# One transformer block and two layers with a top-k expert lookup on one core: query weights of four heads kept in four gather slots

## The chip, the cores and the metric

The program runs on one core of a Trainium2 chip. A core has a matrix engine (TensorE, PE in the profile, with its weight loads as PEld), a vector engine (VectorE, DVE), a scalar engine (ScalarE, ACT), a general engine that issues the gathers (GpSimd, POOL) and one that issues the other transfers (SyncE, SP). Sixteen DMA engines move data between HBM and the on-chip memory (SBUF, 128 partitions). Results of matmuls stand in PSUM. The metric is the device time of one execution in microseconds, and the median over runs is compared.

## The reference

`x` (256 x 1024) goes through one block with differential and grouped attention, then through a product-key expert lookup, and then through two layers with a Fourier branch, windowed attention and a gated feed-forward. Everything is float32. The part that matters here is the lookup:

```python
def one(xc):                      # 128 tokens
    q = (xc @ w_q).reshape(C, PEER_HEADS, 2, PEER_HALF)              # 8 heads, 2 x 128
    s = jnp.einsum('chpd,hpnd->chpn', q, subkeys, ...)
    sv, si = lax.top_k(s, PEER_TOPK)                                 # 16 of 128, twice
    cand = sv[:, :, 0, :, None] + sv[:, :, 1, None, :]
    best, pos = lax.top_k(cand.reshape(C, PEER_HEADS, 256), PEER_TOPK)
    ids = ...                                                        # 16 experts per token and head
    g = jax.nn.softmax(best, axis=-1)
    ue = jnp.take(u, ids, axis=0); ve = jnp.take(v, ids, axis=0)     # rows of 1024 each
    a = jax.nn.gelu(jnp.einsum('cd,chkd->chk', xc, ue), approximate=False)
    return jnp.einsum('chk,chkd->cd', (g * a), ve)
```

Each of 256 tokens and 8 heads takes 16 rows of `u` and of `v`, 4 KB each: 268 MB in all.

## The kernel before

**Stages.** The kernel first does the block (modulation, input projections, attention, output projection, second norm), then 16 stages of the lookup, then the two layers. A stage is one head for one half of the tokens (128 tokens, one to a partition); stage n works on tokens c = n % 2 of head n // 2. `NC` is 2, `PH` 8, `TOPK` 16, `STAGES` 16.

**One stage.** `u` and `v` stand side by side in `uv`, so one gather fetches for each of 128 partitions a row of 2048 floats (8 KB), 1.05 MB in all. POOL issues 16 gathers (`gather`, L759). VectorE takes the dot product of the `u` half with the token (`dot`, L2199, recorded on L2202), 16 times, and after every 4 of them a small product (`weights`). ScalarE does the gelu of those 4 (L1677) and from each weight a diagonal matrix (L1681, four buffers). TensorE multiplies each diagonal matrix with the `v` half and adds it up in PSUM (`experts`, L1159, recorded on L1166), and adds one to `pair_free` when a pair is done. `pair_free` stands at NS = 16 when the first stage begins.

**Slots.** There are NS = 16 slots of 8 KB per partition. Slots 0 to 7 are halves of the four quarters of `ring`, the buffer in which every other weight lands (`pairs_at`, L237); slots 8 to 15 are in `arena`, where the attention kept its data. `FIRST_SLOTS` (L87) says which slot takes gather k of a stage: the five arena slots 8 to 12 first. In the first stage a gather waits for whatever used its slot before; in later ones gather k waits for the same k of the stage before.

**Queries.** Head h needs 1 MB of query weights in `wqb`, which SP loads when the queries of head h - 1 are done (`q_done`, L726 to L729), and TensorE takes them in `all_queries(h)` (L1134) and writes the scores (`all_key_sums`). VectorE finds the 16 best (`topk`), which is needed one stage ahead. ScalarE copies the queries out of PSUM (`query_out`) and does the softmax (`softmax`, L1645), for which another activation table is loaded than for gelu. The orders of the work on each engine are written out by hand, and the middle heads are loops (`Fori`).

**Ends.** The modulation weights come first, in four slots of 2 MB. TensorE sums the first four of eight row blocks in float32 from the raw slot (`mod_raw`, L838, L840). The others are split by ScalarE (`first_high`, L448) and VectorE (`first_rest`, L454) into a high part and a remainder and multiplied in `mod_parts`. In the layers every weight piece of 1024 columns is split in the same way: `weight_high` on ScalarE (L557), `weight_rest` on VectorE (L572). SP loads the first layer slots (`lslot(0)` to `lslot(3)`, the four quarters of `ring`) at L731 to L738, one after the other.

## Time and profile before

| what | value |
|---|---|
| median of 3 runs | 1478.48 us (1478.26 to 1478.79) |
| the profiled execution | 1479.35 us, its span 1477.5 us |
| mean granted TensorE clock | 0.964 |
| busy share: PE, DVE, ACT, POOL | 90%, 73%, 41%, 19% |
| moved by gathers | 268.45 MB, 36,864 packets |
| moved by SP's loads | 146.82 MB |

The shares are means over three stretches. Until 227 us the block is computed, between 227 and about 888 us the lookup, and the rest are the two layers, about 290 us each. The page cuts the span in 40 slices of 37 us, and a share or rate of one slice tells more than the mean. Rates of transfer are over all sixteen DMA engines.

### The profile page before, as it was taken

The page shows a single profiled execution, that of the slowest core. Times are in us where ns is not written, and L with a number is a line of the kernel's source. Part 1 is how long each engine was busy: PE and PEld are TensorE (multiplying, and loading weights), DVE is VectorE, ACT ScalarE, POOL GpSimd, SP SyncE. Part 2 cuts the span into 40 slices and gives each one's busy share as a digit, 9 for nine tenths or more (in the row PEclk, how much of TensorE's full clock was granted, in tenths as well). Part 3 has the DMA queues.
Part 4 walks back from the last instruction along what each step waited for, and adds up shares of the span by engine and source line. Part 5 has one row for each costly group of instructions (what it writes and reads, how often), then busy time and mean ns, then how long its engine had stood idle before and what let it go on. Part 6 is the DMA issues. An engine that isn't in the chain of part 4 may idle for free.

```text
span 1477.5 us, 18644 instructions
## 1 busy us (share of the span) xinstructions
PE 1335.6 (90%) x6216; PEld 917.7 (62%) x6216; DVE 1077.9 (73%) x2271; ACT 601.4 (41%) x1234; POOL 281.5 (19%) x263
## 2 busy tenths in 40 slices
PE   8998899998797979798897788999999999999998
PEld 3876664543342424253343346679999876899987
DVE  5698857876767677776777777878887577788864
ACT  5343643212222222212132226566665455666652
POOL 0000004554433334444444220000000000000000
PEclk9999999999898989899898899999999999999999
DMA  9624437999999999999999996434445433345530
GB/s 395 261 114 170 173 138 324 421 421 422 421 422 422 422 422 422 422 422 422 422 421 422 421 401 258 171 114 172 172 172 200 161 144 126 115 178 195 197 145 29
DMA packets 49847, 416.21 MB, mean 282 GB/s; under 512 B 5488, under 2 KB 5616, under 8 KB 7024
## 3 DMA queue, kind: packets, MB, share of 16 engines
q0 software_dynamic: 36864, 268.45, 43.7%
q1 hardware_dynamic: 12912, 146.82, 26.1%
q8 instruction: 44, 0.72, 0.2%
q14 instruction: 27, 0.22, 0.0%
HBM read 414.20 MB, written 1.05 MB: 281 GB/s over the span
## 4 chain that ended last, share of the span: by engine, by line
PE 54%; DMA 16%; DVE 14%; issue 9%; POOL 5%; ACT 2%; POOLq 0%; DVEq 0%; SPq 0%; ACTq 0%
DMA ring<-in_uv,ids 13%; PE ps L1166 7%; PE ps L1454 6%; PE ps L1453 6%; PE ps L1455 6%; PE ps L1245 4%; PE ps L1247 4%; PE ps L1246 4%; POOL arena L762 3%; POOL ring L762 2%; DVE arena L2202 2%; PE ps L989 2%; PE ps L878 2%; PE ps L880 2%; PE ps L879 2%
## 5 line engine op out<-in xcount | busy, mean ns | idle before, releaser
L1166 PE MATMUL ps<-arena 128*128 128x512 f32 x512 | 254.7, 653 | 93.2 <-ACT arena L1681 92.7
L1166 PEld LDWEIGHTS ps<-arena 128*128 128x128 f32 x512 | 105.2, 210 | 235.5 <-issue 124.8
L572 DVE TENSOR_TENSOR arena_r<-ring,arena_r 128x1024 fp32r<-128x1024 f32 x152 | 185.1, 1223 | 60.7 <-ACT arena_r L557 60.2
L762 POOL DMA_INDIRECT arena<-in_uv,ids x128 | 137.6, 1075 | 479.1 <-issue 256.4
L1166 PE MATMUL ps<-ring,arena 128*128 128x512 f32 x512 | 225.6, 593 | 2.7 <-ACT arena L1681 1.6
L2202 DVE CUSTOM_DVE_ANT_0 ring<-ring,arena 128x1024 f32<-128x1024 f32 x128 | 153.1, 1222 | 70.8 <-DMA ring<-in_uv,ids 67.5
L1453 PE MATMUL ps<-hH,arena_r 128*128 128x256 f32 x704 | 199.4, 283 | 0.0
L1455 PE MATMUL ps<-hH,arena_r 128*128 128x256 f32 x704 | 199.2, 283 | 0.0
L1454 PE MATMUL ps<-arena_r 128*128 128x256 f32 x704 | 199.2, 283 | 0.0
L2202 DVE CUSTOM_DVE_ANT_0 arena<-arena 128x1024 f32<-128x1024 f32 x128 | 153.3, 1224 | 57.1 <-DMA arena<-in_uv,ids 55.0
L557 ACT ACTIVATE arena_r<-ring 128x1024 fp32r<-128x1024 f32 x152 | 158.8, 1052 | 58.8 <-PE ps L1247 58.6
L1166 PEld LDWEIGHTS ps<-ring,arena 128*128 128x128 f32 x512 | 96.9, 190 | 124.5 <-issue 119.0
L762 POOL DMA_INDIRECT ring<-in_uv,ids x128 | 143.3, 1119 | 108.5 <-PE ps L1166 74.5
L1681 ACT ACTIVATE arena<-cst,wts 128x128 f32<-128x128 f32 x256 | 89.5, 394 | 145.7 <-DVE wts L2196 73.6
L1454 PEld LDWEIGHTS ps<-arena_r 128*128 128x128 f32 x704 | 135.2, 192 | 0.0
L1453 PEld LDWEIGHTS ps<-hH,arena_r 128*128 128x128 f32 x704 | 135.2, 192 | 0.0
L1455 PEld LDWEIGHTS ps<-hH,arena_r 128*128 128x128 f32 x704 | 135.2, 192 | 0.0
L1677 ACT ACTIVATE gel<-dots 128x4 f32<-128x4 f32 (+2 forms) x68 | 13.9, 205 | 207.9 <-DVE dots L2202 207.7
L1245 PE MATMUL ps<-arena_r 128*128 128x512 f32 x240 | 94.9, 395 | 1.7 <-DVE arena_r L627 1.6
L1247 PE MATMUL ps<-arena_r 128*128 128x512 f32 x240 | 93.5, 390 | 0.0
L1246 PE MATMUL ps<-arena_r 128*128 128x512 f32 x240 | 93.5, 389 | 0.0
L1837 ACT ACTIVATE arena<-ps,lps 128x256 f32<-128x256 f32 x88 | 49.8, 566 | 96.6 <-DVE arena L2465 56.9
(334 smaller groups left out, 2041.8 us busy)
## 6 DMA issues: line engine op xcount, KB each, us to landing
ring<-in_lw SPq DMA_DIRECT2D x39, 2048.0 KB, 7.7
ring<-in_b1w SPq DMA_DIRECT2D x18, 2048.0 KB, 8.8
wqb<-in_wq SPq DMA_DIRECT2D x8, 1024.0 KB, 9.0
ring<-in_lw SPq DMA_DIRECT2D x8, 1024.0 KB, 5.1
ring<-in_lw SPq DMA_DIRECT2D x2, 1088.0 KB, 10.6
arena<-in_uv,ids POOLq DMA_INDIRECT x128
ring<-in_uv,ids POOLq DMA_INDIRECT x128, 22.0
cst<-in_const SPq DMA_DIRECT2D x1, 1487.5 KB, 22.1
```

The costliest lines, as they stand in the source:

```text
L557: nc.scalar.activation(high_of(l, p), piece_raw(p), ACT.Copy).then_inc(w_hi, 1)
L572: nc.vector.tensor_tensor(low_of(l, p), piece_raw(p), high_of(l, p).bitcast(F32), ALU.subtract)\
L762: pool.indirect_dma_start(pairs_at[at], None, uv, bass.IndirectOffsetOnAxis(ap=ids[:, c, k:k + 1], axis=0))\
L1166: last = nc.tensor.matmul(ps[:, 4 + 2 * c + b, :], diag[:, k % 4, :], vrows[at[k]][:, b * 512:(b + 1) * 512], start=False, stop=(close and ...
L1245: nc.tensor.matmul(dst, ah, high_of(l, p)[:, cols_], start=first, stop=False, skip_group_check=True)
L1246: nc.tensor.matmul(dst, ah, low_of(l, p)[:, cols_], start=False, stop=False, skip_group_check=True)
L1247: last = nc.tensor.matmul(dst, al, high_of(l, p)[:, cols_], start=False, stop=end, skip_group_check=True)
L1453: nc.tensor.matmul(dst, high, hH[:, k, :], start=(k == 0), stop=False)
L1454: nc.tensor.matmul(dst, high, hL[:, k, :], start=False, stop=False)
L1455: last = nc.tensor.matmul(dst, low_of(l, p)[:, k * P:(k + 1) * P], hH[:, k, :], start=False, stop=(k == KD - 1))
L1681: nc.scalar.activation(diag[:, k % 4, :], ident, ACT.Copy, scale=wts[:, c, k:k + 1])\
L2202: V.tensor_tensor_reduce(out=urows[at], in0=urows[at], in1=hrow[:, c, :], scale=1.0, scalar=0.0, op0=ALU.mult, op1=ALU.add, accum_out=dots ...
```

## The change

Six edits stand in one diff.

1. `SLOTS` lists twelve slots, and gather k of stage n takes slot `SLOTS[(16 n + k) % 12]`, so it waits for the pair twelve before it. Slots 8 to 11 take no gathers.
2. These four areas (`kept_wq`) take the query weights of heads 1 to 4. SP loads them when the attention's scores (`sc_done`) and its transposes (`pt_done`) are done. Heads 5 to 7 go through `wqb` as before, the first of them when head 0's queries are done.
3. The loops over heads are written out on all engines.
4. The first four slots of modulation weights are loaded as halves; `mod_raw` waits for the first half (`half_in`), everything else for both.
5. In the head loop ScalarE does the second softmax ahead of `query_out`; at the end of the lookup it loads the table for square roots behind three weight pieces and not ahead of them. SP's loads of the first layer slots wait for the last use of both halves of a quarter.
6. In the layers, `weight_rest` of pieces 5 to 7 stands behind `rotation`, and that of piece 9 behind the two products with `rstd`.

```diff
@@ -84,9 +84,21 @@
 GROUP = 4
-FIRST_SLOTS = (8, 9, 10, 11, 12, 0, 1, 2, 3, 4, 5, 13, 14, 15, 6, 7)
+SLOTS = (12, 3, 0, 1, 2, 4, 5, 13, 14, 15, 6, 7)
+KEPT = 4
 GROUPS = TOPK // GROUP
 STAGES = NC * PH
+
+
+def place(n, k):
+    return SLOTS[(TOPK * n + k) % len(SLOTS)]
+
+
+def turn_of(n, k):
+    return (TOPK * n + k) // len(SLOTS) + 1
+
+
+LAST_USE = {at: g + 1 for g in range(TOPK * STAGES) for at in (SLOTS[g % len(SLOTS)],)}
 ENDS = tuple(GROUP * (g + 1) for g in range(GROUPS))
@@ -237,6 +249,7 @@
         hrow = area(64, NC, D)
+        kept_wq = [area(8 * i, KD, 256) for i in range(KEPT)]
         diag = area(72, 4, P)
@@ -528,7 +543,7 @@
             elif l == 0 and p < 2:
-                act.wait_ge(pair_free, NS + TOPK * (STAGES - 1) + 12)
+                act.wait_ge(q_done, PH)
             elif l == 0 and p < 4:
@@ -711,7 +726,10 @@
                 w = 2048 if n == IN_SLOT[1] else SLOT
-                sp.dma_start(ring[:, n % RING, 0:w], b1w[n, :, 0:w]).then_inc(slot_in[n % RING], 16)
+                at = SLOT // 2 if n < MOD_A else 0
+                if at:
+                    sp.dma_start(ring[:, n, 0:at], b1w[n, :, 0:at]).then_inc(half_in[n], 16)
+                sp.dma_start(ring[:, n % RING, at:w], b1w[n, :, at:w]).then_inc(slot_in[n % RING], 16)
                 if n == 1:
@@ -723,14 +741,18 @@
             sp.dma_start(skb[:, :], sk).then_inc(sk_in, 16)
-            with sp.Fori(1, PH) as h:
-                sp.wait_ge(q_done, h)
-                sp.dma_start(wqb[:, :, :], wq[bass.ds(h, 1), :, :].rearrange("a p (k n) -> (a p) k n", k=KD))\
-                    .then_inc(wq_in, 16)
-
-            sp.wait_ge(pair_in[NS - 2], 16 * STAGES)
+            sp.wait_ge(sc_done, 16)
+            for i in range(KEPT):
+                if i == 2:
+                    sp.wait_ge(pt_done, 16)
+                sp.dma_start(kept_wq[i], wq[i + 1, :, :].rearrange("p (k n) -> p k n", k=KD)).then_inc(kept_in[i], 16)
+            for h in range(KEPT + 1, PH):
+                sp.wait_ge(q_done, 1 if h == KEPT + 1 else h)
+                sp.dma_start(wqb[:, :, :], wq[h, :, :].rearrange("p (k n) -> p k n", k=KD)).then_inc(wq_in, 16)
+
+            sp.wait_ge(pair_in[place(STAGES - 1, TOPK - 2)], 16 * turn_of(STAGES - 1, TOPK - 2))
             for j in range(RING):
-                sp.wait_ge(pair_free, NS + TOPK * (STAGES - 1) + 2 * j + 2)
+                sp.wait_ge(pair_free, NS + max(LAST_USE[2 * j], LAST_USE[2 * j + 1]))
                 if j == 0:
@@ -757,26 +779,23 @@
 
-            def gather(n, c, k, at):
+            def gather(n, c, k):
+
+                at = place(n, k)
                 pool.sem_inc(pool_passed, 1)
...
 
-            def stage(n, c):
-
-                pool.wait_ge(ids_ready, n + 1)
-                pool.sem_inc(pool_passed, 1)
-                for k, at in enumerate(FIRST_SLOTS):
-                    pool.wait_ge(pair_free, TOPK * n + k + 1)
-                    gather(n, c, k, at)
-
             pool.wait_ge(first_ids, 1)
             pool.sem_inc(pool_passed, 1)
-            for k, at in enumerate(FIRST_SLOTS):
+            for k in range(TOPK):
+                at = place(0, k)
                 if k == 8:
                     pool.wait_ge(ids_ready, 1)
-                if at == 0:
+                if k >= len(SLOTS):
+                    pool.wait_ge(pair_free, NS + k - len(SLOTS) + 1)
+                elif at == 3:
                     pool.wait_ge(wo_used, 4)
@@ -784,17 +803,13 @@
                     pool.wait_ge(q_done, 1)
-                gather(0, 0, k, at)
-            stage(1, 1)
-            with pool.Fori(1, PH - 1) as i:
-                stage(i * 2, 0)
-                stage(i * 2 + 1, 1)
-            stage(STAGES - 2, 0)
-            pool.wait_ge(ids_ready, STAGES)
-            pool.sem_inc(pool_passed, 1)
-            for k in range(TOPK):
-                pool.wait_ge(pair_free, TOPK * (STAGES - 1) + FIRST_SLOTS.index(k) + 1)
-                gather(STAGES - 1, 1, k, k)
+                gather(0, 0, k)
+            for n in range(1, STAGES):
+                pool.wait_ge(ids_ready, n + 1)
+                pool.sem_inc(pool_passed, 1)
+                for k in range(TOPK):
+                    pool.wait_ge(pair_free, NS + TOPK * n + k - len(SLOTS) + 1)
+                    gather(n, n % NC, k)
 
@@ -835,7 +850,7 @@
 
-                wait_slot(pe, i)
+                pe.wait_ge(half_in[i], 16)
                 for k in range(4):
@@ -1133,10 +1148,14 @@
 
-                pe.wait_ge(wq_in, 16 * h + 16)
+                if h <= KEPT:
+                    pe.wait_ge(kept_in[h - 1], 16)
+                else:
+                    pe.wait_ge(wq_in, 16 * (h - KEPT + 1))
+                head = kept_wq[h - 1] if h <= KEPT else wqb
                 for s in range(2):
                     for k in range(KD):
-                        last = nc.tensor.matmul(ps[:, 0, s * S:(s + 1) * S], wqb[:, k, s * P:(s + 1) * P], hT[:, k, :],
+                        last = nc.tensor.matmul(ps[:, 0, s * S:(s + 1) * S], head[:, k, s * P:(s + 1) * P], hT[:, k, :],
                                                 start=(k == 0), stop=(k == KD - 1))
@@ -1687,11 +1706,11 @@
             experts(0, 0, groups=range(1, GROUPS))
-            with act.Fori(0, PH - 2) as i:
+            for i in range(PH - 2):
                 softmax(i * 2 + 2, 0)
                 experts(i * 2 + 1, 1)
+                softmax(i * 2 + 3, 1)
                 query_out(i + 2)
-                softmax(i * 2 + 3, 1)
                 experts(i * 2 + 2, 0)
@@ -1702,8 +1721,6 @@
 
-            table(ACT.Sqrt)
-
             def squares_of(c):
@@ -1711,6 +1728,7 @@
             weight_high(act, 0, 0, 1, 2)
+            table(ACT.Sqrt)
             block_high(act, 1, range(4))
@@ -2196,18 +2214,19 @@
 
-            def dot(n, c, k, at):
-
-                dve.wait_ge(pair_in[at], 16 * n + 16)
+            def dot(n, c, k):
+
+                at = place(n, k)
+                dve.wait_ge(pair_in[at], 16 * turn_of(n, k))
                 V.tensor_tensor_reduce(out=urows[at], in0=urows[at], in1=hrow[:, c, :], scale=1.0, scalar=0.0,
...
 
-            def products(n, c, ends=ENDS, at=FIRST_SLOTS):
+            def products(n, c, ends=ENDS):
 
...
                     for k in range(start, end):
-                        dot(n, c, k, at[k])
+                        dot(n, c, k)
                         if k == start and g > 0:
@@ -2320,8 +2337,6 @@
 
-                weight_rest(dve, l, *range(5, P_O - 2))
-
                 def rotation(i, gain):
@@ -2349,16 +2364,18 @@
                 rotation(1, lpv(l, "kn"))
+                weight_rest(dve, l, *range(5, P_O - 2))
                 fold_fourier()
...
                 variance(20, HD)
-                weight_rest(dve, l, P_O - 2, P_O - 1)
+                weight_rest(dve, l, P_O - 2)
                 newton(20, l * 4 + 8)
...
                     run(V.tensor_tensor(r3, r3, rstd[:, r0:r0 + nh].unsqueeze(2).broadcast_to([P, nh, HD]), ALU.mult))
+                weight_rest(dve, l, P_O - 1)
                 for c in range(NC):
```

The loops on TensorE and VectorE are written out in the same way (`for i in range(...)` in place of `Fori`), and `experts` takes its slot from `place(n, k)`.

On GpSimd, the first gathers of the lookup, before: `first_ids`, `wo_used`, `ids_ready`, `mod_used`, `q_done` are what a gather waits for, and `arena` and `ring` say in which kind of slot it lands.

```order
9 L762 DMA arena<-in_uv,ids 128x2048 [waits first_ids]
10 L762 DMA arena<-in_uv,ids 128x2048 x4
11 L762 DMA ring<-in_uv,ids 128x2048 [waits wo_used]
12 L762 DMA ring<-in_uv,ids 128x2048 x2
13 L762 DMA ring<-in_uv,ids 128x2048 [waits ids_ready]
14 L762 DMA ring<-in_uv,ids 128x2048 [waits mod_used]
15 L762 DMA ring<-in_uv,ids 128x2048
16 L762 DMA arena<-in_uv,ids 128x2048 [waits q_done]
17 L762 DMA arena<-in_uv,ids 128x2048 x2
18 L762 DMA ring<-in_uv,ids 128x2048 [waits mod_used]
```

The same place on GpSimd in the changed kernel, up to the first gather that waits for a freed pair:

```order
9 L786 DMA arena<-in_uv,ids 128x2048 [waits first_ids]
10 L786 DMA ring<-in_uv,ids 128x2048 [waits wo_used]
11 L786 DMA ring<-in_uv,ids 128x2048 x3
12 L786 DMA ring<-in_uv,ids 128x2048 [waits mod_used]
13 L786 DMA ring<-in_uv,ids 128x2048
14 L786 DMA arena<-in_uv,ids 128x2048 [waits q_done]
15 L786 DMA arena<-in_uv,ids 128x2048 [waits ids_ready]
16 L786 DMA arena<-in_uv,ids 128x2048
17 L786 DMA ring<-in_uv,ids 128x2048 [waits mod_used]
18 L786 DMA ring<-in_uv,ids 128x2048
19 L786 DMA arena<-in_uv,ids 128x2048 [waits pair_free]
```

Before, five gathers stand ahead of the first that waits for the output projections (`wo_used`); now one does, and the thirteenth already waits for a pair.

On SyncE, from the last loads of the block to the first layer slots, before (`wqb` and `skb` are the queries' and keys' weights, `pair_in14` the landing in slot 14; the loop of L726 runs seven times):

```order
20 L723 DMA wqb<-in_wq 128x2048 [waits modcol_done]
21 L725 DMA skb<-in_sk 128x2048 [waits in_used]
22 L726 UNCONDITIONAL_BRANCH
23 L728 ISA [waits q_done]
24 L728 DMA wqb<-in_wq 128x2048
25 L726 REGISTER_ALU
26 L726 COMPARE_AND_BRANCH
27 L735 DMA ring<-in_lw 128x2048 [waits pair_free,pair_in14]
28 L736 DMA ring<-in_lw 128x2048
```

The same on SyncE in the changed kernel (`pair_in0` is the landing in slot 0, gather 14 of the last stage):

```order
26 L741 DMA wqb<-in_wq 128x2048 [waits modcol_done]
27 L743 DMA skb<-in_sk 128x2048 [waits in_used]
28 L748 DMA arena<-in_wq 128x2048 [waits sc_done]
29 L748 DMA arena<-in_wq 128x2048
30 L748 DMA arena<-in_wq 128x2048 [waits pt_done]
31 L748 DMA arena<-in_wq 128x2048
32 L751 DMA wqb<-in_wq 128x2048 [waits q_done] x3
33 L757 DMA ring<-in_lw 128x2048 [waits pair_free,pair_in0]
34 L758 DMA ring<-in_lw 128x2048
```

Four loads of query weights moved to the attention's end and three stay behind `q_done`; the first layer load now waits in `pair_free` for pair 256, the last of all, where it waited for the second pair of the last stage.

## Rows read from the trace of the kernel before

**Rows 1.** The page, rate of transfer in 40 slices of 37 us.
```profile
GB/s 395 261 114 170 173 138 324 421 421 422 421 422 422 422 422 422 422 422 422 422 421 422 421 401 258 171 114 172 172 172 200 161 144 126 115 178 195 197 145 29
```
**Rows 2.** Transfer queues in 390 to 750 us: packets, MB, share of 16 engines.
```profile
q0 software_dynamic: 20281, 147.69, 98.5%
q1 hardware_dynamic: 576, 4.19, 2.8%
```
**Rows 3.** Timeline, VectorE (start, length), the last dots of stages 4 and 5.
```profile
442.40 1.23 DVE L2202 CUSTOM_DVE_ANT_0 ring<-ring,arena 128x1024 f32<-128x1024 f32 x1 [1.25 <-DMA ring<-in_uv,ids]
...
482.12 1.23 DVE L2202 CUSTOM_DVE_ANT_0 ring<-ring,arena 128x1024 f32<-128x1024 f32 x1 [1.25 <-DMA ring<-in_uv,ids]
```
**Rows 4.** Timeline, TensorE, the last transposes of the attention's probabilities.
```profile
201.59 0.60 PE L956 MATMUL ps<-cst,arena 128*128 128x128 f32 x4
```
**Rows 5.** Stretches: length, busy us and count of each engine, PEclk, DMA share, GB/s.
```profile
210.00:227.00 17.00, 16.10 (x78) 10.29 (x79) 13.13 (x54) 6.12 (x14) 0.00 (x0) 1.00 0.00 1
...
229.00:231.00 2.00, 2.00 (x6) 0.94 (x5) 1.83 (x8) 0.10 (x1) 1.55 (x2) 1.00 0.72 164
```
**Rows 6.** Timeline, GpSimd, the first and the sixth gather.
```profile
227.75 1.08 POOL L762 DMA_INDIRECT arena<-in_uv,ids  x1 [226.61 <-issue]
...
234.54 1.36 POOL L762 DMA_INDIRECT ring<-in_uv,ids  x1 [0.30 <-issue]
```
**Rows 7.** The chain of waits: TensorE behind the output projections.
```profile
233.56 4.45 PE ps L813 x11
```
**Rows 8.** Issue to landing: the sixth gather alone, then all of L762.
```profile
ring<-in_uv,ids POOLq DMA_INDIRECT x1, 12.1
...
DMA to landing us min/median/max: 9.4/22.0/25.0
```
**Rows 9.** Timeline, GpSimd at the first freed pair of stages 5 and 6, and TensorE.
```profile
466.88 0.94 POOL L762 DMA_INDIRECT arena<-in_uv,ids  x1 [13.30 <-PE ps L1166]
...
508.07 0.94 POOL L762 DMA_INDIRECT arena<-in_uv,ids  x1 [13.95 <-PE ps L1166]
...
472.86 10.46 PE L1166 MATMUL ps<-ring,arena 128*128 128x512 f32 x24
```
**Rows 10.** Timeline, ScalarE, the table load ahead of gelu in stage 6.
```profile
501.26 1.28 ACT L1677 ACT_TABLE_LOAD   x1
```
**Rows 11.** The chain of waits at the start; then a stretch as in rows 5.
```profile
3.62 20.20 DMA ring<-in_b1w
23.87 6.24 PE ps L840 x8
...
24.00:26.00 2.00, 2.00 (x3) 0.26 (x2) 1.97 (x6) 1.85 (x2) 0.00 (x0) 0.50 0.99 426
```
**Rows 12.** Timeline, VectorE, after the remainders of the third slot.
```profile
31.85 0.54 DVE L1949 TENSOR_SCALAR arena<-ps,sm 128x256 f32<-128x256 f32 x1 [3.24 <-ACT arena_r L1523]
```
**Rows 13.** The chain of waits, the first weights of layer 0.
```profile
885.64 5.05 DMA ring<-in_lw
```
**Rows 14.** Timeline at the join: VectorE, TensorE, VectorE.
```profile
888.12 1.23 DVE L2202 CUSTOM_DVE_ANT_0 arena<-arena 128x1024 f32<-128x1024 f32 x1 [0.75 <-DMA arena<-in_uv,ids]
...
890.33 1.98 PE L1166 MATMUL ps<-arena 128*128 128x512 f32 x4 [0.36 <-ACT arena L1681]
...
892.91 1.23 DVE L572 TENSOR_TENSOR arena_r<-ring,arena_r 128x1024 fp32r<-128x1024 f32 x1 [3.07 <-ACT arena_r L557]
```
**Rows 15.** Timeline of layer 0: VectorE, VectorE, ScalarE.
```profile
911.26 3.50 DVE L572 TENSOR_TENSOR arena_r<-ring,arena_r 128x1024 fp32r<-128x1024 f32 x3 [2.46 <-ACT arena_r L557]
...
918.89 1.21 DVE L2354 TENSOR_REDUCE sm<-arena 128x16 f32<-128x1024 f32 x1
...
917.22 1.04 ACT L1752 ACTIVATE arena<-arena 128x1024 f32<-128x1024 f32 x1
```
**Rows 16.** Queues in 866 to 876 us, and VectorE's longest wait in it.
```profile
q14 instruction: 1, 0.01, 0.2%
...
873.30 1.22 DVE L2202 CUSTOM_DVE_ANT_0 arena<-arena 128x1024 f32<-128x1024 f32 x1 [2.29 <-DMA arena<-in_uv,ids]
```

More of the change, by code:

```diff
@@ L324, in program @@
         slot_in = [sem(f"slot_in{i}") for i in range(RING)]
+        kept_in = [sem(f"kept_in{i}") for i in range(KEPT)]
+        half_in = [sem(f"half_in{i}") for i in range(MOD_A)]
         act_step, dve_step, passed, pool_passed = sem("act_step"), sem("dve_step"), sem("passed"), sem("pool_passed")
@@ L1181, in _ @@
             keys(2)
-            with pe.Fori(1, PH - 2) as i:
+            for i in range(1, PH - 2):
                 experts(i * 2, 0)
@@ L2223, in _ @@
             for k in range(GROUP):
-                dot(0, 0, k, FIRST_SLOTS[k])
+                dot(0, 0, k)
             dve.wait_ge(prob_done, 1)
@@ L2230, in _ @@
             for k in range(GROUP, TOPK):
-                dot(0, 0, k, FIRST_SLOTS[k])
+                dot(0, 0, k)
                 if k % 4 == 0 and k > GROUP:
@@ L2236, in _ @@
             dve.wait_ge(row_out, 4)
-            with dve.Fori(0, PH - 1) as i:
-                chain.enter(i, 2 * (4 * 3 + 1 + 7 + 1))
+            for i in range(PH - 1):
                 topk(i * 2 + 2, i + 1, 0)
@@ L2242, in _ @@
                 products(i * 2 + 2, 0)
-                chain.leave(PH - 1)
             dve.wait_ge(mod_out, MODS)
```

10 lines of the change are left out of this document (5 added, 5 removed).

## The prediction, written before the changed kernel was run

> **What bounds the kernel now.** I read the slices of the page first. From about 227 us to 885 us the transfers stand at 421 to 422 GB/s without a break [rows 1], and between 390 and 750 us the gathers alone fill 98.5% of the sixteen engines [rows 2]. A gather is 128 rows of 8 KB, 1.05 MB, so it costs 1.0486/0.422 = 2.485 us of this stream, and so does each head's 1 MB of query weights that goes through it. One head (two stages of 16 gathers and one weight load) is 33 x 2.485 = 82.0 us. VectorE shows the same: the last gather of one stage lands at 442.40, that of the next at 482.12 [rows 3], 39.7 us apart, 16 x 2.485. In this stretch no engine's work has a price unless it leaves the stream empty; bytes and starts have. Before and behind it the chain of waits runs through TensorE, VectorE and ScalarE.
>
> **Removed bytes.** Seven weight loads stand in the stream (heads 1 to 7). Afterwards it holds three (heads 5 to 7); the other four go out once the attention scores and transposes are done. The last attention transposes end at 202.2 [rows 4], and between 210 and 227 us the transfers run at 1 GB/s [rows 5]: 4 MB fit in with room. Gain: 4 x 2.485 = **-9.9 us**. No query waits for them, as these land well before 227.
>
> **The first gathers.** Now five gathers go into the arena before anything from the ring is needed (POOL issues from 227.75, every 1.24 us, and the sixth at 234.54 without having waited [rows 6]). Afterwards only one does; the second goes to slot 3, which is free when both output projections are done. TensorE's next work starts at 233.56 [rows 7], and POOL follows a release by 0.8 us: 234.4. The stream really fills up 2.4 us after the first issue (164 GB/s in 229 to 231, 0 before, [rows 5]), at about 230.2. The gather of 234.54, sixth in line, lands 12.1 us later [rows 8], at 246.6; 230.2 + 6 x 2.485 is 245.1, so completion adds 1.5, and a gather that finds the stream empty lands after 2.4 + 2.5 + 1.5 = 6.4 us. The second gather then lands at 240.8 and not at 230.2 + 2 x 2.485 + 1.5 = 236.7: **+4.1 us**. If the second start is as quick as the queue latency inside a busy stream it could be 2, not less than 1.5; and not over 5.
>
> **Twelve slots and not sixteen.** Gather k of a stage is now let go by the pair twelve before. The tight ones are k = 12 to 15, which wait for the stage's own first four pairs. In the odd stage shown, the previous stage's last gather landed at 442.40, and POOL issued what the first freed pair released at 466.88, 24.5 us later [rows 3, 9]; gather 12 is due 13 x 2.485 = 32.3 us after 442.40. It has 7.8 us, against the 6.4 just worked out, and the three behind it are freed every 1.74 us (24 matmul records for six pairs in 10.46, [rows 9]) and due every 2.49. In the even stage POOL comes 508.07 - 482.12 = 26.0 later [rows 3, 9], but there the softmax stands behind the copy of the queries, and so the softmax, its table load and gelu's table load of 1.28 us, which ends at 502.54 [rows 10], all fall between the dots and gelu. With the softmax ahead of the copy one load of 1.28 and the 0.4 of the softmax leave this path, and 24.3 us remain. So the stream stays full, with 1.4 us to spare: **0**. What is not known is the lead a transfer needs with only three ahead of it; the smallest that the trace shows is 9.4 us, the median 22.0 [rows 8], and both are queueing. That is the rival below. Moving the softmax has no other price: TensorE's key sums wait for the copy, but its next pair waits for gelu anyway.
>
> **First weights as halves.** The third slot of modulation weights lands at 3.62 + 20.20 = 23.82 and TensorE's eight row sums start on it at 23.87; they take 6.24 us [rows 11]; between 24 and 26 us the granted clock is 0.50, the level of 1.2 GHz, after TensorE had stood still for 1.8 us. The first half lands 2.5 us earlier, at 21.3. Then they are done by 27.6 even at the lower clock. Whole slots are still awaited by ScalarE's splitting, so VectorE's remainders don't move; but VectorE idles 3.24 us until 31.85 for ScalarE, which waits for TensorE behind these sums [rows 12]. That idle time is what can go: **-3.2 us**, 2.4 if the clock falls all the same, 0 if a later transfer sets the end (the trace has no DMA wait between 40 and 227, so I take 3.2). It shifts everything up to the first gather.
>
> **The join to layer 0.** This is what the new order costs. 256 gathers over twelve slots end on slots 12, 3, 0, 1. Slots 0 and 1 are the ring quarter of the first layer weights, and SP issues all four quarters in order. Now SP issues at 885.64, before the last pair is even read, and the first MB lands 5.05 us later [rows 13], 2.6 after the last dot began at 888.12. Afterwards it must wait for the last pair's matmuls, 890.33 + 1.98 = 892.3 [rows 14], so it lands at 892.4 + 5.05 = 897.4 on the old clock. VectorE's remainder of the first piece stands ahead of the residual in program order and starts 1.1 us behind ScalarE's start on it: 898.6 and not 892.91 [rows 14], **+5.7 us**. The table load moved behind three pieces gains nothing, since there is no data at that time. TensorE now stands still for 7.7 us instead of 2 and may start at the lower clock; its work there is paced by VectorE (2.7 us a piece), so I count 0, at most 2.
>
> Where a rule stands beside this: the Trainium skill (TensorE: Matmul & The Clock Gate, "HAM oscillation — how this bites in real kernels") says that a DMA wait of some microseconds sends TensorE back to the lower clock. By it the join would cost up to 2 more. The row of 24 to 26 us agrees that a pause has that effect.
>
> **Reordered remainders.** Layer by layer VectorE idles 2.46 us until 911.26 for ScalarE; the four rotation products (1.7 us) move in front of that wait. The norm's reduction starts at 918.89, ScalarE's square for it ends at 918.26 [rows 15]. So 0.6 is to be had, less 0.2 for the last piece that now comes later to TensorE: **-0.8 us** for both layers (-1.4 to 0).
>
> **Unrolled loops.** The loops hold their code: in 390 to 750 us no instruction queue appears among the queues [rows 2]. Written out, some 3,000 further instructions must be fetched through the same engines. At 64 bytes that is 0.2 MB, 0.5 us of stream if spread. 
> **Sum:** -9.9 + 4.1 - 3.2 + 5.7 - 0.8 + 1.0 = -3.1 us. The profiled execution took 1479.35 (span 1477.5), 0.9 over the median of 1478.48, so I forecast 1479.35 - 3.1 = 1476.2 for one like it and **1475.4** for the median. 0.2% is 3.0 us, about what can be told from no change, so the forecast lies on that edge.
>
> **Rivals.** (1) *The stream is cheaper than thought:* the second start costs 2 and not 4, fetches cost nothing, TensorE's earlier end carries over. -9.9 + 2 - 3.2 + 5.7 - 1.4 = -6.8: 1471.7. For it: the second start falls on engines already warm. Against: the join is arithmetic. (2) *Twelve slots starve the stream (slower):* in each of 13 stages gather 12 arrives late by what its lead exceeds 7.8 us. At 8.6 us it is 0.8 x 13 = 10.4, 1478.5 - 3.1 + 10.4 = 1485.8; at the 9.4 of rows 8 it is 21, 1496. It decides from 8.0 us on. For it: no gather in the trace had a lead under 9.4. Against: those were queued behind others, and 6.4 follows from the first six. The Trainium skill (DMA: Bandwidth & Descriptors, "Anatomy of one DMA — SWDGE (gpsimd) path") gives 2.0 us plus size over 436 GB/s, 4.4 us for a gather; by that the margin is 3.4 and this rival falls. (3) *The join and the fetches are dearer* (2 for the clock, 5 for fetches): -3.1 + 2 + 4 = +2.9: 1481.4. (4) *The early part does not carry over*, the weights' halves being hidden: +3.2, 1478.6, which I count with (3).
>
> **Chances.** Forecast 0.60 (its own range 1472.5 to 1478; 0.36 of it faster, 0.24 within 0.2%), (1) 0.17 faster, (2) 0.12 slower, (3) and (4) 0.11 (0.06 within, 0.05 slower). Faster 0.53, same 0.30, slower 0.17. The range 1469.5 to 1483 reaches into (1) and (3) and leaves out most of (2).
>
> **What would show it.** VectorE's wait of 3.24 us near 30 us gone and the first gather near 224.5; the second gather 6.6 us behind it; three weight loads after 240; 422 GB/s in every slice of the stream, and no waits for a landing longer than 1.3 us; the last dot near 879; first layer weights landing 9.3 us behind the last dot's start and not 2.6; the layers shorter by under 1 us. A stream below 420 GB/s in the middle would make the forecast wrong upward, a first gather still at 227.7 by 3 us.

## The result: 0.17% slower, and the profile after

The changed kernel takes 1481.45 us (median of 20 runs, 1480.51 to 1482.94), the kernel before in the same sessions 1478.88 (20 runs, 1478.26 to 1480.3). The ratio is 1.0017 with a 95% interval of 1.0011 to 1.0024: slower by some 2.6 us, where the forecast was 3.1 us faster. The profiled span is 1480.3 us against 1477.5, 2.8 us more, and I split them at four points.

| stretch | before | after | change | forecast |
|---|---|---|---|---|
| start to first gather's issue | 227.75 | 224.57 | -3.2 | -3.2 |
| to the last dot of stage 1 | 317.18 | 315.56 | +1.6 | +4.1 - 2.5 |
| to the last dot of all | 888.12 | 885.17 | -1.3 | -7.5 + 1.0 |
| to the first remainder of layer 0 | 892.91 | 896.80 | +6.8 | +5.7 |
| to the end of the span | 1477.5 | 1480.3 | -1.1 | -0.8 |

Columns two and three are where the stretch ends. The second point in both kernels, in VectorE's timeline, before and then after:

```profile
317.18 1.22 DVE L2202 CUSTOM_DVE_ANT_0 ring<-ring,arena 128x1024 f32<-128x1024 f32 x1 [1.24 <-DMA ring<-in_uv,ids]
...
315.56 1.23 DVE L2221 CUSTOM_DVE_ANT_0 arena<-arena 128x1024 f32<-128x1024 f32 x1 [1.25 <-DMA arena<-in_uv,ids]
```

The first two lines and the last came close to what was worked out; the fourth cost 1.1 us more. The third is where the forecast broke: three weight loads of 2.485 us are gone from it, and it is shorter by 1.3 us only.

The early part, in timelines of the kernel after (start, length, idle before and its releaser):

```profile
28.47 0.99 DVE L1967 TENSOR_SCALAR arena<-ps,sm 128x256 f32<-128x256 f32 x2
...
224.57 1.08 POOL L786 DMA_INDIRECT arena<-in_uv,ids  x1 [223.44 <-issue]
231.21 0.94 POOL L786 DMA_INDIRECT ring<-in_uv,ids  x1 [5.55 <-PE ps L1004]
```

The wait of 3.24 us at 31.85 [rows 12] is gone; the same operation now follows its predecessor at 28.47 without a wait. The first gather goes out 3.2 us earlier than in [rows 6], and the second stands 5.55 us behind TensorE's output projection.

The transfers, from the page, then from the queues in 390 to 750 us, then stretches (length, busy time and count of PE, PEld, DVE, ACT, POOL, granted clock, DMA share, GB/s):

```profile
GB/s 392 263 114 209 157 226 317 421 421 422 421 421 418 421 411 422 412 411 421 418 420 409 413 349 257 170 115 163 180 171 192 158 119 160 114 176 192 199 145 29
```

```profile
q0 software_dynamic: 20322, 148.00, 99.4%
q1 hardware_dynamic: 288, 2.10, 1.4%
q8 instruction: 6, 0.10, 0.1%
q14 instruction: 10, 0.08, 0.1%
```

```profile
390.00:750.00 360.00, 297.56 (x763) 144.10 (x763) 253.81 (x631) 84.27 (x217) 148.99 (x141) 0.94 1.01 417
...
816.00:850.00 34.00, 25.89 (x53) 11.29 (x54) 24.08 (x51) 6.51 (x21) 13.75 (x12) 0.80 1.01 412
```

In [rows 1] every slice of the stream shows 421 or 422; now there are slices of 409 to 413. In [rows 2] no instruction queue appears; now two do, with 16 packets and 0.18 MB, which is 0.4 us of stream. The bytes are nothing, and yet 1% of the rate is missing. In the landing times of the gathers there is a regular step of 2.49 us. Eight times between 390 and 888 us one gather of the changed kernel lands 0.94 to 0.97 us later than this step, and the following ones keep the delay. Each stands 2.1 to 3.3 us behind an 8 KB packet of instructions on q14:

```
fetch on q14 (us)   403.9  452.3  524.1  571.0  646.6  696.9  769.6  818.0
next late landing   406.24 454.40 527.41 573.04 648.63 699.31 772.29 820.63
later by            0.97   0.97   0.97   0.94   0.97   0.97   0.95   0.96
```

Six other 8 KB packets on q14 in this stretch (445.9, 471.9, 607.4, 653.4, 765.9 and 831.0 us) have no step behind them. The trace of before has one such step between 390 and 888 us, that of [rows 16], and one more at 330.5; the changed kernel has a small one of 0.27 at 335.7. So the table's third stretch has six full steps and 0.27 more than before, 6.0 us, against the 6.2 by which -1.3 misses the three loads' -7.5. So far this is a coincidence in time; whose fetches they are, and whether twelve slots matter, was for the experiments.

The join, in the chain of waits of the kernel after, and VectorE's timeline:

```profile
869.20 21.28 PE ps L1185 x47
890.54 5.15 DMA ring<-in_lw
895.72 1.06 ACT arena_r L572
```

```profile
885.17 1.23 DVE L2221 CUSTOM_DVE_ANT_0 ring<-ring,arena 128x1024 f32<-128x1024 f32 x1 [0.70 <-DMA ring<-in_uv,ids]
...
896.80 1.23 DVE L587 TENSOR_TENSOR arena_r<-ring,arena_r 128x1024 fp32r<-128x1024 f32 x1 [9.91 <-ACT arena_r L572]
...
915.21 3.50 DVE L587 TENSOR_TENSOR arena_r<-ring,arena_r 128x1024 fp32r<-128x1024 f32 x3 [0.98 <-ACT arena_r L572]
```

The load leaves 5.4 us behind the start of the last dot; in [rows 13, 14] it left 2.5 us ahead of it. VectorE stands for 9.91 us where it stood for 3.07. Further on its wait of 2.46 us [rows 15] is 0.98.

### The profile page after: what moved, and what is told of

It is laid out like the page before. It is cut to its first block, busy times and chain, and to the rows that moved or that the text cites. A ratio compares the mean times of both kernels' runs of the same rounds, so it can differ in the third digit from the quotient of the medians.

```text
span 1480.3 us, 17546 instructions
## 1 busy us (share of the span) xinstructions
PE 1335.9 (90%) x6216; PEld 916.7 (62%) x6216; DVE 1076.5 (73%) x2271; ACT 598.9 (40%) x1234; POOL 279.4 (19%) x263
## 3 DMA queue, kind: packets, MB, share of 16 engines
q0 software_dynamic: 36864, 268.45, 43.9%
## 4 chain that ended last, share of the span: by engine, by line
PE 52%; DVE 22%; DMA 13%; issue 6%; ACT 3%; POOL 3%; DVEq 0%; SPq 0%; POOLq 0%; ACTq 0%
DMA ring<-in_uv,ids 8%; PE ps L1185 7%; PE ps L1472 6%; PE ps L1474 6%; PE ps L1473 6%; PE ps L1264 4%; DMA arena<-in_uv,ids 4%; PE ps L1266 4%; PE ps L1265 4%; DVE ring L2221 4%; DVE arena L2221 3%; POOL ring L786 2%; PE ps L1004 2%; PE ps L893 2%; PE ps L894 2%
## 5 line engine op out<-in xcount | busy, mean ns | idle before, releaser
L1185 PE MATMUL ps<-ring,arena 128*128 128x512 f32 x684 | 315.5, 612 | 33.2 <-ACT arena L1700 33.2
L2221 DVE CUSTOM_DVE_ANT_0 ring<-ring,arena 128x1024 f32<-128x1024 f32 x171 | 205.7, 1223 | 99.4 <-DMA ring<-in_uv,ids 99.2
L1185 PEld LDWEIGHTS ps<-ring,arena 128*128 128x128 f32 x684 | 133.7, 197 | 207.1 <-issue 163.3
L1185 PE MATMUL ps<-arena 128*128 128x512 f32 x340 | 169.3, 638 | 65.7 <-ACT arena L1700 65.7
L786 POOL DMA_INDIRECT ring<-in_uv,ids x171 | 184.2, 1077 | 192.3 <-PE ps L1185 147.1
L786 POOL DMA_INDIRECT arena<-in_uv,ids x85 | 94.7, 1114 | 394.4 <-issue 237.3
L1185 PEld LDWEIGHTS ps<-arena 128*128 128x128 f32 x340 | 66.9, 203 | 157.2 <-ACT arena L1700 82.5
L2221 DVE CUSTOM_DVE_ANT_0 arena<-arena 128x1024 f32<-128x1024 f32 x85 | 103.4, 1222 | 42.2 <-DMA arena<-in_uv,ids 41.4
```

The lines of the kernel that those rows point to most:

```text
L786: pool.indirect_dma_start(pairs_at[at], None, uv, bass.IndirectOffsetOnAxis(ap=ids[:, c, k:k + 1], axis=0))\
L1185: last = nc.tensor.matmul(ps[:, 4 + 2 * c + b, :], diag[:, k % 4, :], vrows[place(n, k)][:, b * 512:(b + 1) * 512], start=False, stop=(clo ...
L2221: V.tensor_tensor_reduce(out=urows[at], in0=urows[at], in1=hrow[:, c, :], scale=1.0, scalar=0.0, op0=ALU.mult, op1=ALU.add, accum_out=dots ...
```

## The experiments

Theory A: the instruction fetches of POOL's written-out loop delay the stream. Theory B: twelve slots starve it. Theory C: only both together. All kernels below were timed against the kernel before; the interval is that of the ratio.

### Is it POOL's code, the depth, both, or the other engines' code?

**e1**, the kernel before with POOL's loop written out:

```diff
-            with pool.Fori(1, PH - 1) as i:
+            for i in range(1, PH - 1):
```

> The kernel before with one edit: POOL's loop over the stages is written out, every other engine keeps its loop, sixteen slots. Theory A (each 8 KB instruction fetch that POOL needs for its written-out gathers puts a lasting 0.95 us into the landings of the gathers; the trace after shows eight such steps, the trace before two): about seven fetches more, 6 to 7 us slower than before, so about +0.45%, and the landings go up in steps of some 0.95 us about every 1.5 stages. Theory B (the twelve slots starve the stream, the fetches are harmless): no change, ratio 1.000. Theory C (fetches cost only together with the shallower queue): fetches appear in the trace with steps in the single landings, but the span stays within 1 us.

Measured: 1478.73 us against 1478.96, ratio 1.0000 (0.9991 to 1.0009). Its queues in 390 to 750 us and its stretch of 816 to 850 us:

```profile
q14 instruction: 2, 0.02, 0.0%
```

```profile
816.00:850.00 34.00, 24.93 (x55) 10.65 (x54) 24.88 (x56) 8.05 (x23) 8.72 (x8) 0.85 1.01 421
```

Three fetches in the whole loop (443.6, 603.7, 764.4), not the seven of the expectation, and no step behind any. Theory A falls: the eight steps of the changed kernel are not POOL's.

**e2**, the kernel before, loops and sixteen slots kept, with every gather held back by four more pairs (the first stage's last four and the last stage alike):

```diff
-                    pool.wait_ge(pair_free, TOPK * n + k + 1)
+                    pool.wait_ge(pair_free, TOPK * n + k + 5)
```

> The kernel before with one edit: sixteen slots and all loops as they are, but every gather from the thirteenth of the first stage on waits for four pairs more, so that at most twelve are in flight or in use, as in the changed kernel. Theory A (fetches of the written-out loop): no change beyond 0.5 us. Theory B (twelve slots starve the stream): 6 us slower, about +0.4%. Theory C (both together): no change here, slow packets rare.

Measured: 1480.17 us, ratio 1.0007 (0.9998 to 1.0016). The profile has the last dot of stage 1 at 318.61 (before: 317.18), that of stage 3 at 401.56 (400.17) and the last of all at 889.89 (888.12). So the depth costs 1.4 us in the first two stages and 0.4 in the 490 us behind them. Theory B, with 6 us, falls.

**e3**, both edits:

> The kernel before with both edits: POOL's loop written out and twelve pairs at most in flight or in use. Theory A: as with the written-out loop alone, +6 to 7 us. Theory B: as with the depth alone, +6 us. Theory C (interaction): +6 us here although each alone costs under 1 us; if both cost by themselves, the sum of the two.

Measured: 1480.70 us, ratio 1.0008 (0.9999 to 1.0017): 1.7 us, which the interval doesn't tell from the depth's 1.2 alone. Theory C falls in this form. One of POOL's fetches does leave a step here, 0.60 us at 615.00, behind the fetch at 612.34; the shares below say why.

**e4**, the kernel before with the four other loops written out (PE, ACT, DVE and, not shown, SP), POOL's kept:

```diff
-            with pe.Fori(1, PH - 2) as i:
+            for i in range(1, PH - 2):
...
-            with act.Fori(0, PH - 2) as i:
+            for i in range(PH - 2):
...
-            with dve.Fori(0, PH - 1) as i:
-                chain.enter(i, 2 * (4 * 3 + 1 + 7 + 1))
+            for i in range(PH - 1):
...
-                chain.leave(PH - 1)
```

> The kernel before with one edit: the loops of PE, ACT, DVE and SP over the stages are written out, POOL keeps its loop. Theory A (only POOL's fetches delay, since the steps stand behind fetches that come once in 1.5 stages, which fits POOL's stream): no change beyond 1 us. Its rival (the fetches of the other engines delay the stream too, or stall PE, ACT and DVE at the end of a stage): 2 to 5 us slower.

Measured: 1484.97 us, ratio 1.0047 (1.0033 to 1.0060), 6.0 us more in the medians. All eight steps are in its landings, at the same gathers as in the changed kernel. So it is another engine's code, with loops alone, sixteen slots and all seven loads.

### Which engine

**e5, e6, e7**: the same with PE's, DVE's or ACT's loop alone.

> The kernel before with PE's loop over the stages alone written out. With all loops but POOL's written out the kernel was 0.47% slower, and its trace has all eight steps of 0.95 us in the landings at the same gathers as the changed kernel. Theory D1 (one engine's fetches all lie on one DMA engine, whose share of every gather falls behind by about 0.95 us a fetch; that engine is PE): +6 us and the eight steps here, none in the two kernels with DVE's or ACT's loop written out. Theory D2 (the fetches of all engines add up, in whatever place): about +2 us here and as much in each of the other two.

> The kernel before with DVE's loop over the stages alone written out. If DVE's fetches are the ones behind the steps (about 128 instructions every 1.5 stages would fit DVE, with 16 dots, their waits and the selection of a stage): +6 us and the eight steps here, nothing in the PE and ACT kernels. If it is PE or ACT: no change. If fetches of all engines add up: about +2 us.

> The kernel before with ACT's loop over the stages alone written out. If ACT's fetches are the ones behind the steps: +6 us and the eight steps here, nothing in the PE and DVE kernels. If it is PE or DVE: no change. If fetches of all engines add up: about +2 us.

Measured: PE 1479.05 us, ratio 1.0005 (0.9996 to 1.0014); DVE 1486.10, ratio 1.0048 (1.0034 to 1.0062); ACT 1478.72, ratio 1.0001 (0.9992 to 1.0010), each against 1478.48. It is VectorE's code alone that costs. The kernel with DVE's loop written out, queues in 390 to 750 us, then stretches:

```profile
q0 software_dynamic: 20260, 147.53, 98.5%
q1 hardware_dynamic: 576, 4.19, 2.8%
q14 instruction: 6, 0.05, 0.0%
```

```profile
487.00:652.00 165.00, 135.93 (x334) 64.90 (x333) 113.88 (x281) 37.33 (x96) 67.84 (x63) 0.91 1.01 422
652.00:816.00 164.00, 137.42 (x337) 65.51 (x336) 114.21 (x283) 38.18 (x97) 68.45 (x65) 0.91 1.01 422
816.00:850.00 34.00, 24.05 (x50) 10.10 (x49) 24.84 (x66) 8.73 (x22) 7.25 (x8) 0.80 0.86 355
```

And the kernel with PE's written out, the same two views:

```profile
q8 instruction: 6, 0.10, 0.1%
```

```profile
816.00:850.00 34.00, 24.55 (x51) 10.36 (x51) 24.63 (x56) 7.86 (x22) 7.86 (x8) 0.85 1.01 421
```

PE fetches more bytes (0.10 MB against 0.05) and costs nothing that can be measured. DVE's eight fetches (408.3 to 827.7 us) each bring a step of 0.94 to 0.97; its last dot stands at 894.89, 6.8 us later than before, seven more steps than before's one. Note where the rate shows it: it stays at 422 GB/s until 816 us while the landings are already 6 us late, and then drops to 355.

**Where the step arises.** The gathers' 36,864 packets are 144 for each gather, 128 of 8 KB and 16 of 4 bytes, and the trace tells of a gather's landing by sixteen increments of its semaphore. I take them as its sixteen shares; the gather has landed with the last. In the kernel with DVE's loop written out they stand so (us):

```
landing of the gather         407.17 410.62 461.32 536.84 582.54 658.14 708.84 781.89 830.08 857.32
last share behind the next      0.59   1.56   2.53   3.48   4.44   5.48   6.46   7.44   8.45   3.26
that one behind the first       2.57   2.57   2.61   2.60   2.64   2.65   2.66   2.68   2.66   0.54
```

One share alone falls behind, by about 1 us with each of the eight fetches, and the other fifteen stay together and run ahead into the slots that are free. That is why the rate stays at 422 GB/s until 816 us. It drops between 840 and 856 us, to 243 and 279 GB/s in its two halves, when they have run 8.4 us ahead, and POOL has waited 22.49 us for a freed pair (20.2 at most in the trace of before, where the rate stays at 421 to 422). In the changed kernel, with twelve slots, the last share is 2.0 to 2.7 us behind from the second step on and gets no further, but for three gathers beside weight loads (up to 3.9); there the same loss shows sooner, as slices of 409 to 413 GB/s from 518 us on. The packets agree: each of DVE's eight fetches takes 0.33 us, and as it ends one 8 KB packet of the gathers starts that takes 0.97 us where the others take 0.31; 0.33 + 0.65 is the step.

The other engines' fetches push a share back too, but not the last one. Matching the increments before and behind a fetch, fifteen keep their places and one moves (us ahead of the last share, before and after the fetch):

```
PE, e5     3.11 to 1.64   3.16 to 1.63   3.12 to 1.57   2.00 to 0.44   2.99 to 1.37   1.64 to 0.09
POOL, e1   2.09 to 1.40   1.39 to 0.69   0.72 to 0.05
ACT, e7    2.36 to 1.65   1.67 to 0.99
```

DVE's fetches meet a share that is already the last, so each costs its full 0.97. POOL's three meet one share that stood 2.1 us ahead, and use up just that; in e3 it stood only 0.7 us ahead, and there the second fetch made the step of 0.60. PE's move a share by 1.5 to 1.6 us each, but the first five meet shares with time to spare, and the sixth leaves its share 0.1 us short of the last. So a fetch of any engine has a price, and whether a landing shows it depends on how much the share has left. The trace doesn't name the DMA engine of a packet: that a share is one DMA engine, always the same for DVE, is inferred from the places that add up.

**e11**, the kernel before with DVE looping over four pairs of stages and the last three written out:

```diff
-            with dve.Fori(0, PH - 1) as i:
+            with dve.Fori(0, 4) as i:
...
-                chain.leave(PH - 1)
+                chain.leave(4)
+            for i in range(4, PH - 1):
```

> The kernel before in which DVE loops over four pairs of stages and has the last three pairs written out (with all seven written out it was 7 us slower). If each fetch of DVE costs by itself: no step before about 640 us, then four steps of 0.95 us, and about 3.5 us slower than before. If the cost is in the first fetches only or in something else of the written-out loop (fewer instructions of the loop's chain, another timing of the dots): either no change or the whole 7 us.

Measured: 1482.09 us, ratio 1.0024 (1.0015 to 1.0033), 3.4 us. The first fetch is at 619.1, and the four steps are at 621.48, 697.03, 745.28 and 795.96 us. The last falls where VectorE waits for each landing, so its timeline shows it:

```profile
792.52 1.22 DVE L2202 CUSTOM_DVE_ANT_0 ring<-ring,arena 128x1024 f32<-128x1024 f32 x1 [0.16 <-DMA ring<-in_uv,ids]
795.98 1.22 DVE L2202 CUSTOM_DVE_ANT_0 ring<-ring,arena 128x1024 f32<-128x1024 f32 x1 [2.08 <-DMA ring<-in_uv,ids]
```

Two dots of neighbouring gathers are 3.46 us apart, not 2.49. Half the fetches, half the price: the cost is per fetch, as long as the share that they meet is the last.

### The other terms

**e8**, the kernel before without four of the weight loads; the four heads then use the first head's query weights, so this part of the computation is left out:

```diff
-            with sp.Fori(1, PH) as h:
+            with sp.Fori(1, 5) as h:
+                sp.wait_ge(q_done, h)
+                sp.sem_inc(wq_in, 16)
+            with sp.Fori(5, PH) as h:
```

> The kernel before, its loops and sixteen slots kept, in which SyncE leaves out the loads of the second to fifth head's query weights and only signals them (the heads use the first head's weights: that part of the computation is changed). It measures the term of the prediction for four weight loads out of the stream by itself. By the prediction's sum: -9.9 us, about -0.67%. Its rival (the loads were hidden in gaps between gathers): under 2 us.

Measured: 1468.24 us, ratio 0.9935 (0.9922 to 0.9949), 10.2 us less in the medians. In its profile 650.6 us lie between the first gather's issue (225.77) and the last dot (876.32), and 660.4 in the one of before: 9.8 us less. The term of -9.9 was right.

**e12**, the kernel before with the parts that need no twelve slots (halves; softmax ahead of the query copy; table load behind three pieces; remainders reordered), their diff as in the change:

> The kernel before with only those parts of the change that need neither twelve slots nor written-out loops: the first four weights as halves, the order of softmax and query copy, the table load and the remainders' order. By the prediction's terms -3.2 and -0.8 us: about 1474.9 us, 0.27% faster than before and faster than the changed kernel by 6.5 us. Rival (what the early part gains is given back before the last dot): 1478 to 1479 us.

Measured: 1474.17 us, ratio 0.9974 (0.9964 to 0.9985), 4.6 us less. Its first layer load is issued at the landing of the last gather but one, and VectorE's first remainder stands 3.6 us behind the last dot's start (886.37) where it stood 4.8 behind in [rows 14]:

```profile
883.90 4.96 DMA ring<-in_lw
888.89 1.06 ACT arena_r L558
889.98 1.23 DVE arena_r L573
```

So the moved table load is worth 1.2 us when the weights are on time; I had it at nothing, as it is with twelve slots.

**e9**, the changed kernel with another order of the slots:

```diff
-SLOTS = (12, 3, 0, 1, 2, 4, 5, 13, 14, 15, 6, 7)
+SLOTS = (12, 13, 14, 3, 0, 1, 2, 4, 5, 15, 6, 7)
...
-                elif at == 3:
-                    pool.wait_ge(wo_used, 4)
+                elif at == 13:
+                    pool.wait_ge(o_tile, 4)
+                elif at == 14:
+                    pool.wait_ge(wo_used, 4)
...
-                elif at == 13:
+                elif at == 15:
```

> The changed kernel with one edit: the twelve slots go round in the order 12, 13, 14, 3, 0, 1, 2, 4, 5, 15, 6, 7 instead of 12, 3, 0, 1, 2, 4, 5, 13, 14, 15, 6, 7; slot 13 waits for the transposes of the attention rows (done before the first gather's issue), slot 14 for the output projection. If the join and the wait of the second gather cost what the prediction says: the third instead of the second gather waits for the projection (about -2.5 us), and slots 0 and 1 are free nine pairs before the end, so the first layer weights are asked for at the last landings and not after the last pair (about -5.5 us): 8 us faster than the changed kernel, about 1473.5 us, 0.35% under the kernel before. Rival (the weights for layer 0 then share the stream with the last gathers, or the last dots' chain sets the end anyway): 2 to 4 us of it stay away.

Measured: 1474.22 us, ratio to before 0.9974 (0.9963 to 0.9984), and 7.2 us under the changed kernel's median. POOL's timeline, then the chain of waits:

```profile
223.93 1.08 POOL L786 DMA_INDIRECT arena<-in_uv,ids  x1 [222.80 <-issue]
225.32 0.94 POOL L786 DMA_INDIRECT arena<-in_uv,ids  x1 [0.30 <-issue]
230.54 0.94 POOL L786 DMA_INDIRECT arena<-in_uv,ids  x1 [4.28 <-PE ps L1006]
```

```profile
881.38 4.96 DMA ring<-in_lw
886.36 1.07 ACT arena_r L572
887.45 1.22 DVE arena_r L587
```

The second gather no longer waits, the third does, and the layer's weights are asked for at 881.38 and not at 890.54. From the last dot (883.81) to the first remainder it is 3.6 us instead of 11.6: the join gives back 8.0. The last dot comes only 1.4 us earlier than in the changed kernel, 0.6 of it from the first gather. The second start did give its 2.5: from the first landing to the fourth it is 10.08 us here (229.44 to 239.52) and 12.63 in the changed kernel. But 1.95 of it are lost again at the seventeenth gather, the first of stage 1. POOL issues it here (first line) hardly earlier than in the changed kernel (second line), since it waits for a freed pair in both:

```profile
270.07 0.96 POOL L786 DMA_INDIRECT ring<-in_uv,ids  x1 [7.28 <-PE ps L1187]
...
270.71 0.95 POOL L786 DMA_INDIRECT ring<-in_uv,ids  x1 [8.36 <-PE ps L1185]
```

In e9 the landing before it is at 272.53 and its own at 276.97, 4.43 us apart and not 2.49: here twelve slots do leave the stream empty. In the changed kernel it lands at 278.02, 2.49 us behind its predecessor. The eight steps are still there. It beats the kernel before and equals e12, which keeps all seven loads; e9 without VectorE's fetches was not built, and by the 6 us that they cost it would take about 1468 us, an estimate.

**e10**, the changed kernel with DVE in a loop of two passes over six stages (the least common period of twelve slots and two chunks), to save fetches:

```diff
-            for i in range(PH - 1):
+            with dve.Fori(0, 2) as j:
+                chain.enter(j, 3 * 2 * (4 * 3 + 1 + 7 + 1))
+                for u in range(3):
+                    i = j * 3 + u
...
+            for i in range(6, PH - 1):
```

> The changed kernel with one edit: DVE's stages stand in a loop of two passes over six stages each, and the last two stages behind it, instead of fourteen written out. If code that was fetched in the first pass is kept for the second: three of the eight steps of 0.95 us go, about 3 us faster than the changed kernel (1478.5 us). If a body of six stages is too long to be kept and is fetched again on each pass: no change from the changed kernel (1481.5 us).

Measured: 1489.49 us, ratio to before 1.0081 (1.0067 to 1.0095): 8 us slower than the changed kernel; neither expectation held. Where the loop goes back, in the timelines of VectorE and POOL, and as a stretch:

```profile
525.05 0.30 DVE L2151 MAX8 sval<-ps 128x8 f32<-128x128 f32 x1 [5.56 <-issue]
...
529.94 0.09 DVE L2153 MATCH_VALUE_LOAD sidx<-sval,ps 128x8 f32 x1 [1.92 <-issue]
```

```profile
549.10 1.58 POOL L786 DMA_INDIRECT ring<-in_uv,ids  x1 [20.24 <-PE ps L1185]
```

```profile
517.00:554.00 37.00, 19.02 (x40) 7.85 (x39) 24.53 (x64) 7.58 (x19) 10.87 (x10) 0.77 0.81 327
```

The second pass fetches its code again, and VectorE stands for 5.56 and 1.92 us with no releaser, with the selection in front of the next dots. The pairs come late, POOL waits 20.24 us for a slot, and the stream drops to 327 GB/s. Three fetches fall into these 10 us (522.9, 527.9, 532.9).

## Why the prediction was wrong

**Removed bytes (-9.9): right.** e8 alone measured 10.2 in the medians and 9.8 in the profile, and the three loads left are issued at 242.51, 573.50 and 657.33 us.

**The first gathers (+4.1): right.** From the first landing to the fourth the changed kernel takes 12.63 us (230.21 to 242.84), the one before 8.45 (233.22 to 241.67): 4.2 more. The second gather went out at 231.21, 6.6 behind the first, as worked out, while a gather alone took 5.64 us from issue to landing (224.57 to 230.21), where I had 6.4.

**Twelve slots (0): right for this kernel, partly by luck.** The same depth costs 1.2 us in e2, nearly all in the first two stages, which the argument from stages 5 and 6 did not look at. In the changed kernel it costs little there: from the fourth landing to that of stage 1's last gather 0.6 us are left beside 28 gathers and one weight load. Its gathers come later by the late second start, and so find freed pairs; e9, which starts sooner, pays 1.95 us. Rival (2), with its cost in each of 13 stages, fell.

**Halves (-3.2): right in kind, its exact size luck.** The wait is gone, and the granted clock of 24 to 26 us is now 0.81 where it was 0.50 [rows 11]. But the first gather's issue varies between profiles: 225.3 to 228.0 us in the ten kernels with the early part as before, 223.9 to 225.7 in the four with halves. By the medians of the two groups (227.1 and 224.4) the gain is 2.7. It carried over to the end, so rival (4) fell.

**The join (+5.7): right in kind, 6.8 in size.** I counted the load's issue at 4.3 us behind the start of the last dot; it was 5.4. TensorE still had a backlog of pairs, 21 us of matmuls in one piece. The two microseconds kept for TensorE's lower clock were not spent: from the first remainder to the norm's reduction it takes 25.4 us in the changed kernel (896.80 to 922.23) and in e9 (887.45 to 912.90) alike, although the granted clock was 1.00 in e9 (887 to 897 us) and 0.66 in the changed kernel:

```profile
895.00:905.00 10.00, 6.82 (x26) 5.49 (x26) 7.83 (x12) 7.95 (x15) 0.00 (x0) 0.66 1.01 430
```

So the clock had no price there, as the prediction had it.

**Reordered remainders (-0.8): right**, -1.1.

**Unrolled loops (+1.0): the step that failed.** I wrote that a fetch sits on one engine and a gather lands with its slowest, which the shares bear out, and had the row for it [rows 16]: VectorE waited 1.04 us longer there than its usual 1.25. But then I summed the bytes, 0.5 us of stream if spread, and took +1.0. The row's price times the number of VectorE's fetches was the sum to make. The number was to be had too: 16 dots and 21 steps of the selection, each with its wait, and the weights are some 85 instructions a stage, so at the 64 bytes that the prediction took for an instruction an 8 KB block lasts one and a half stages; the eight fetches are 59 us apart in the mean, which is 1.5 stages. In the stretch of the table they and the small step are 6.0 us more than before. With 6.2 as the table has it in place of 1.0, 6.8 in place of 5.7 and the reorder at -1.1, the sum is +2.9, and the profile shows 2.8. The prediction's own sign for this, a stream below 420 GB/s in the middle, stands in the page.

My end of 5 for this term was too low. Rival (3) gave 1481.4 us, just what was measured, but by luck: its 2 us for the clock were not spent, and the fetches and the join cost 1.2 and 1.1 more than it had.

The Trainium skill (Runtime: NRT & Kernel Launch, "Instruction fetch mechanics") calls the cost of passing into new code "mostly hidden" and prefers unrolling, as a taken branch out of the window stalls. e10 agrees with the stall: 5.56 and 1.92 us. e6 doesn't agree with the other half: written-out code that never stalled its own engine cost the stream 7 us. And the short loop of before, two stages long, shows neither: no instruction queue in 390 to 750 us [rows 2].

**What stays open.** Why the packet behind a fetch takes 0.97 us for DVE's and 0.66 to 0.85 for the others', and by what rule an engine's fetches get their share: DVE's met the same one each time, POOL's in e1 seem to, PE's mostly another. Why DVE's share was the last one was not looked into either, nor whether it could be made to lead.

## What to carry to other kernels

In a stretch that the transfers bind, written-out code is a transfer too: count its fetches, at the delay that one fetch shows in the landings, and not by bytes. A fetch that leaves no step has still used up what its share had left, so that more of them, or a shallower queue as in e3, can bring the step. Keep the loop that fits, or write out only the engines whose fetches leave no step, and look at landings and not at the rate, which stays full until the slots are used up. In a ring of buffers, choose the order so that what the next phase needs first comes free well before the last use; here that order was worth 7 us, nearly all of it at the join.

## What the runs showed of the hardware that was not expected

- An 8 KB instruction fetch of VectorE, 0.33 us long, moves the landings of all later gathers by 0.94 to 0.97 us, since it holds up the one sixteenth of each gather that lands last anyway (e6).
- Fetches of PE (16 KB) hold up one sixteenth by 1.5 us, those of POOL and ACT (8 KB) by 0.7. With sixteen slots this moved no landing, as these sixteenths had more than that left (e5, e1, e7); in e3 one of POOL's moved it by 0.60.
- One sixteenth of the gathers can lag by 7.5 us behind the others with the mean rate still at 422 GB/s (e6, until 816 us); it comes out later as a drop (355 GB/s in 816 to 850 us with sixteen slots).
- A loop body of six stages is fetched again on its second pass, with VectorE standing for 7.5 us in all where it goes back (e10); a body of two stages is not (no instruction queue in 390 to 750 us, [rows 2]).
